# Two layers of attention and experts: row norms by a diagonal product, a first gather with a table of its own, and a later request for four weight blocks

## The reference

```python
def layer(x, mod, P, l, ctx=None):
    sh1, sc1, g1, sh2, sc2, g2 = jnp.split(mod, 6, axis=-1)
    h = rms_norm(x, P["norm_attn_pre"][l]) * (1 + sc1) + sh1
    a, new_ctx = token_mix(h, P, l, ctx)
    x = x + g1 * rms_norm(a, P["norm_attn_post"][l])
    h = rms_norm(x, P["norm_ffn_pre"][l]) * (1 + sc2) + sh2
    x = x + g2 * rms_norm(moe(h, P, l), P["norm_ffn_post"][l])
    return x, new_ctx
```

## Time and profile before

| | us |
| --- | --- |
| median of three runs | 1719.44 (1718.69 to 1720.09) |
| the profiled execution's own time | 1719.05 |
| its span, first to last instruction | 1717.2 |
| PE busy in it | 1671.3 (97%) |
| DVE, ACT, POOL busy | 432.0, 321.0, 121.2 |
| mean granted TensorE clock | 0.994 of full speed |

### The profile page before, as it was taken

How to read it: one execution, slowest core, us unless ns; L and a number is a source line. 1 busy time by engine, 2 the same in 40 slices (tenths; PEclk the granted TensorE clock), 3 DMA queues, 4 the chain that set the end, 5 groups by cost and what they waited for, 6 DMA issues and landing times. The chain is left out here.

```text
span 1717.2 us, 20998 instructions
## 1 busy us (share of the span) xinstructions
PE 1671.3 (97%) x8091; PEld 894.8 (52%) x8091; DVE 432.0 (25%) x1179; ACT 321.0 (19%) x754; POOL 121.2 (7%) x161
## 2 busy tenths in 40 slices
PE   6999999989999999999999999999899999999997
PEld 4778788543333333333367878884333333333332
DVE  1114444351111111111131444434311111111113
ACT  1010341121111111111120113402111111111111
POOL 3001000010000000001020000001100000000000
PEclk8999999999999999999999999999999999999999
DMA  9994233369999999999999632334899999999993
GB/s 388 397 407 155 87 110 129 123 233 405 424 424 424 426 425 426 425 425 425 420 392 420 263 108 98 101 137 161 305 415 427 425 426 425 423 427 423 426 426 136
DMA packets 60381, 559.87 MB, mean 326 GB/s; under 512 B 12941, under 2 KB 13089, under 8 KB 20353
## 3 DMA queue, kind: packets, MB, share of 16 engines
q1 hardware_dynamic: 45360, 529.55, 75.0%
q0 software_dynamic: 14928, 29.02, 4.9%
HBM read 576.02 MB, written 4.78 MB: 338 GB/s over the span
## 5 line engine op out<-in xcount | busy, mean ns | idle before, releaser
L1038 PE MATMUL PS<-ring,region 128*64 128x512 f32 x2048 | 450.6, 592 | 1.9 <-issue 1.5
L1038 PEld LDWEIGHTS PS<-ring,region 128*64 128x64 f32 x2048 | 147.3, 137 | 290.7 <-issue 290.6
L617 PE MATMUL PS<-region,ring 128*128 128x256 f32 x1088 | 245.4, 381 | 0.5 <-DMA ring<-in_blocks 0.5
L1085 PE MATMUL PS<-region 128*128 128x512 f32 x512 | 241.0, 594 | 0.0
L1062 PE MATMUL PS<-ring,region 128*64 128x512 f32 x1024 | 235.5, 602 | 0.2
L617 PEld LDWEIGHTS PS<-region,ring 128*128 128x128 f32 x1088 | 203.8, 190 | 34.2 <-issue 6.3
L1757 DVE SCALAR_TENSOR_TENSOR region<-region,PS 128x256 f32<-128x256 f32 x64 | 26.9, 421 | 670.6 <-ACT region L1320 670.6
L510 PEld LDWEIGHTS PS<-const,region 128*128 128x128 f32 (+1 forms) x925 | 106.8, 141 | 121.8 <-issue 74.1
L510 PE MATMUL PS<-const,region 128*128 128x128 f32 (+1 forms) x925 | 138.5, 279 | 18.2 <-DMA region<-in_c 8.7
L1062 PEld LDWEIGHTS PS<-ring,region 128*64 128x64 f32 x1024 | 68.1, 137 | 158.7 <-issue 158.0
L1324 ACT ACTIVATE region<-PS 128x512 f32<-128x512 f32 x128 | 76.4, 597 | 267.4 <-PE PS L1062 267.4
(11 more groups left out here) (260 smaller groups left out, 985.4 us busy)
## 6 DMA issues: line engine op xcount, KB each, us to landing
ring<-in_expert_blocks SPq DMA_DIRECT2D x192, 2048.0 KB, 16.7
ring<-in_blocks SPq DMA_DIRECT2D x120, 1024.0 KB, 19.7
region<-post_rows POOLq DMA_DIRECT2D x8, 512.0 KB, 5.3
h_table<-region POOLq DMA_DIRECT2D x4, 512.0 KB, 4.0
region<-in_w_kvk POOLq DMA_DIRECT2D x2, 640.0 KB, 18.2
region<-in_mla_w_ukv POOLq DMA_DIRECT2D x2, 512.0 KB, 21.4
region<-in_post_pack POOLq DMA_DIRECT2D x2, 512.0 KB, 24.7
region<-h_table,region POOLq DMA_INDIRECT x64, 10.7
```

What stands on the lines that cost most here:

```text
L617: last = pe.matmul(PS[:, j % 2, m * T:(m + 1) * T], w[:, k, m * P:(m + 1) * P], hT[:, k, :], start=(k == 0), stop=(k == KC - 1))
L1038: last = pe.matmul(PS[e * CAP:(e + 1) * CAP, 0, :], xe[:, k, e * CAP:(e + 1) * CAP], w[:, k % 4, :], start=(k == 0), stop=(k == KC - 1), s ...
L1085: last = pe.matmul(PS[:, 4 + 2 * t + half, :], hot[:, t * P:(t + 1) * P], og[:, half * HALF:(half + 1) * HALF], start=False, stop=True, sk ...
```

## The change

The change has eight parts.

1. **Products with a diagonal.** DVE no longer multiplies the rows by the root. It multiplies a 128 x 128 identity by it (`root_diagonal`), and PE makes the product of a 128 x 128 piece of x with that diagonal in place of the transpose. ACT's sums of squares are made over halves of 512 columns. Where both tiles are ready together (start of layer 1, behind the experts), their roots are made in one chain of nine steps on two columns (`both_roots`).
2. **Residual rows.** `take_gains` multiplies the PSUM rows by the gains, half by half and before the root is known; `add_rows` then multiplies by the root and adds in one instruction per half.
3. **Tile 0 earlier.** Tile 0's product with its diagonal stands inside the output projection, behind step 3 of the last group of eight.
4. **The first gather.** The rows of h are also written to a second table without gates, and the first gather reads that table and waits only for those two writes. Its gates come by a product with the 0/1 matrix that gives its row numbers. The later gathers wait for all writes (`gates_in`).
5. **The first pair's order on PE.** The lists are transposed inside the first gate-and-up product, behind its second step; the second pair's rows are transposed ahead of and around the hidden rows of the first.
6. **The shared expert** is cut at other places between router, gates and first gather.
7. **The end.** x of both tiles is stored in halves as DVE makes them; the addition on POOL is gone.
8. **The later request.** In layer 0 SP waits before block 8 until block 5 has landed.

The parts of the diff that these stand on, cut:

```diff
                 for n in range(LOADS):
+                    if l == 0 and n == L_QA[0]:
+                        sp.wait_ge(ring_in[L_MOD[1] + 1], 16)
                     load_block(n)
...
+                    pool.dma_start(first_table[P * t:P * (t + 1), :], h2x[:, t, 0:D]).then_inc(table_in, 16)
+                    pool.dma_start(table[P * t:P * (t + 1), 0:D], h2x[:, t, 0:D]).then_inc(gates_in, 16)
...
-                pool.wait_ge(table_in, (l + 1) * 64)
+                pool.wait_ge(table_in, (l + 1) * 32)
...
                         if g == 1:
+                            pool.wait_ge(gates_in, (l + 1) * 64)
                             pool.wait_ge(rows_ready, q + 1)
...
-            pool.wait_ge(last_scaled, 1)
-            pool.tensor_tensor(xr[:, 0, :], xr[:, 0, :], moe_scaled[:, 0, :], ALU.add).then_inc(last_ready, 1)
...
-                        last = transpose(PS[:, bank + c // 4, (c % 4) * P:(c % 4 + 1) * P], src[:, t, c * P:(c + 1) * P])
+                        last = pe.matmul(PS[:, bank + c // 4, (c % 4) * P:(c % 4 + 1) * P], xr[:, t, c * P:(c + 1) * P], diag[:, t, :],
+                                         start=True, stop=True)
...
+                            if t == 1 and half == 1 and k == 3:
+                                normalised(1, 0, diag2, 0)
...
+                    for t in range(2):
+                        last = pe.matmul(PS[:, 1, 2:4], first_hot[:, t, :], h2x[:, t, D:D + 2], start=(t == 0), stop=(t == 1), skip_group_check=True)
+                    last.then_inc(first_done, 1)
...
+                                if g == 0 and k == 2 and e == 0:
+                                    transpose_lists()
...
-                    transpose_lists()
                     gate_up(0)
+                    transpose_inputs(1, 0)
                     transpose_hidden(0)
-                    transpose_inputs(1, 0)
+                    transpose_inputs(1, 1)
                     down(0)
-                    transpose_inputs(1, 1)
...
+                def root_diagonal(r, t, diag):
+
+                    ve.tensor_scalar(diag[:, t, :], ident, r, ROOT_SCALE, ALU.mult, ALU.mult).then_inc(xn_ready, 1)
...
+                def take_gains(i, t, rows, rows_in):
+
                     dve.wait_ge(postb_in, (l * 2 + rows_in) * 2 * 16)
+                    for half, cols in enumerate(HALVES):
+                        dve.wait_ge(sum_done, l * SUMS + 2 * i + half + 1)
+                        step.add(ve.tensor_tensor(rows[:, t, cols], PS[:, 4 + 2 * t + half, :], postb[:, t, cols], ALU.mult))
+
+                def add_rows(r, t, rows, done):
+
+                    for half, cols in enumerate(HALVES):
+                        ve.scalar_tensor_tensor(out=xr[:, t, cols], in0=rows[:, t, cols], scalar=r, in1=xr[:, t, cols], op0=ALU.mult, op1=ALU.add).then_inc(done, 1)
```

213 lines of the change are left out of this document (118 added, 95 removed).

## The result

The changed kernel takes 1709.36 us (median of 5 runs, 1708.11 to 1710.63), the kernel before 1719.44 (5 runs): a ratio of 0.9942, 95% interval 0.9927 to 0.9956, or -10.1 us where -4.35 was forecast and 1711.8 us was the lower end of the range. The direction was right, the size was not.

The account below looks back on a forecast made before the run. PE, busy 97% of the span, was taken as the bound, with DMA also full at both layers' starts. The terms 0 - 0.95 - 1.75 + 0.45 - 2.1 = -4.35 us, from 1719.44, gave 1715.1 us; range 1711.8 to 1719.

Parts of the forecast that it names:

- Start of layer 0, 0: Layer 0 up to block 20: waits of 1.54 us swallow the longer products, the deferral is hidden; 0, bounds -0.3 to +1.
- Rival D: Start of layer 0: deferring block 8 starves the load queue, all 5 us show; +0.65 us, 1720.1 us, chance 0.05.
- First pair of layer 0, -2.5: Output projection to second pair, layer 0: fewer PE waits and the new order start the second pair at 387.8; -2.5 us.
- The second gather's lag: Second pair's rows, issued at 377.0 in layer 0: assumed to land after 5.6 us, and 6.7 us in layer 1.
- Gate products, +0.45: Last pair of each layer: the next pass's gate products also stand on PE, +0.45 us per layer.
- Start of layer 1: Block 7 to DVE's scaling: earlier landing, longer products; a lead of 2.05 us becomes 0.95, bounds 0.5 and 1.7.
- First pair of layer 1: Same steps as in layer 0, but the clock falls again; second pair at 1231.5 instead of 1233.27, -1.75 us.
- rival B: First pairs: the clock stays up in both layers; -1.65 us more, 1713.4 us, chance 0.12.
- The end, -2.1: Last stage: without POOL's addition holding DVE up, x is complete at 1712.6 instead of 1714.78; -2.1 us.
- The diagonals: Both norms: eight products with the diagonal cost PE 0.78 us more than eight transposes.
- Rival A: Layer 1's start: transfers keep PE's gain, block 7 lands as before; -3.3 us, 1716.1 us, chance 0.25.
- Rival C: First pairs: the second gather lands late (11.7 us), holding PE and down(0); +5.75 us, 1725.2 us, chance 0.05.

Follow-up runs that it names:

- e1: Changed kernel with the deferral alone undone, so block 8's request no longer waits for block 5 in layer 0: 1709.75 us, ratio 0.9940 to the kernel before.
- e4: Changed kernel with 32 idle transposes on PE ahead of the second pair of layer 0 only: 1712.69 us, ratio 0.9971 to the kernel before.
- e9: Changed kernel with the same 32 idle transposes on PE ahead of the seventeenth pair of layer 0: 1712.75 us, ratio 0.9960 to the kernel before.
- e12: Changed kernel with the first pair's first two slots given back only when the second gather has landed: 1712.95 us, ratio 0.9964 to the kernel before.
- b2: Kernel before with 14 idle transposes in PE's wait for the first pair's hidden rows, both layers: 1717.11 us, ratio 0.9990 to the kernel before.
- e5: Changed kernel with POOL adding the first tile again in the last stage: 1714.77 us, ratio 0.9974 to the kernel before.
- e11: Changed kernel with scaled rows and transposes in place of diagonals and products for both norms: 1705.84 us, ratio 0.9919 to the kernel before.
- e7: Changed kernel with scaled rows and transposes for the second norm only, in the new places: 1706.13 us, ratio 0.9924 to the kernel before.
- e3: Changed kernel with the first pair's order on PE put back to the old one: 1720.04 us, ratio 1.0002 to the kernel before.
- e2: Changed kernel without the first gather's own table; it reads the common table after the gate columns are written: 1712.37 us, ratio 0.9954 to the kernel before.
- e8: Changed kernel with the first tile's diagonal products put behind the output projection: 1714.85 us, ratio 0.9971 to the kernel before.
- e14: e3 with 18 and 14 idle transposes put into PE's two waits in the first pair: 1715.05 us, ratio 0.9974 to the kernel before.
- e10: Changed kernel with the second pair's inputs transposed behind the first pair's down product: 1716.45 us, ratio 0.9982 to the kernel before.
- e13: e11 with 5 and 4 idle transposes in the first pair's two waits: 1705.38 us, ratio 0.9916 to the kernel before.

## Why the prediction was off, point by point

In the prediction's own terms the profiles give 0 - 3.0 - 5.5 + 0.4 - 2.6 = -10.7 us for its 0 - 0.95 - 1.75 + 0.45 - 2.1 = -4.35.

- **Start of layer 0, 0:** 0.08 earlier. The landing of block 20 set it, as described, and the deferral is worth nothing (e1). Rival D did not come. But the 2.4 us that the longer products were to cost ahead of it, and that the waits were to swallow, were not put to the test. They rested on a clock at 0.50 there; in after it was 1.00 from 8 to 26 us, and each tile's products took 2.05 us. Tile 0's cost 0.1 us more than its transposes at the lower clock had, and not 1.8. The clock was up before the products began (modulation for the block ahead of them took 1.07 us, 1.94 before), so it was not the products that kept it up.
- **First pair of layer 0, -2.5:** -3.3. The stage to the first gathered rows gave 2.2 us, where the prediction had 1.2 to 1.3. It counted PE's waits of 0.77 and 0.66 us and left out three others on the way: 0.23, 0.47 and 0.36 us (the last two for ACT and for the first gather). In after one of 0.24 is left.
- **The second gather's lag, taken over from before (5.6 and 6.7 us), is the step behind both this and the largest error below.** It landed after 4.2 us in layer 0 and 4.5 in layer 1. So PE waited 0.59 us for it and not 1.6. "This wait replaces the one for the hidden rows" failed with it: there was a wait of 0.82 us for them, and they set the start of down(0), at 383.46 and not 384.25.
- **Gate products, +0.45:** from the second pair to the end of the pairs, 472.98 us before and 473.40 after: +0.42.
- **Start of layer 1, mis-sized:** the step "block 7 lands 1.2 to 2.4 us earlier; I take 1.6" failed. It landed 3.4 us earlier, as much as the second pair came earlier. The landing did not keep the first release's lead but that of the second pair's start: the queue had slack until then (DMA share 0.77 to 0.98 from 376 to 400 us in the kernel before). e4, e9 and e12 bear that out. The working behind block 7 held (6.25 us worked out, 6.13 measured to DVE's scaling). Worth 2 us.
- **First pair of layer 1, the largest error:** -5.5 within this stage where -1.75 was forecast. 2.5 us come before the first gathered rows (forecast 1.2); of the three waits left out, the one for the first gather was 0.91 us here. The step "PE's idle gap is 1.6 to 2.9 us in either layer now, and it was 2.1 in both before, so I keep each as it was" failed, through the gather's lag: there was no such gap. Before, PE stood 2.06 us without a break; after, there are 0.86 and 0.65 us with the second pair's transposes between. The clock did not fall: 1.65 us, rival B in layer 1, which had a chance of 0.12. b2 confirms that the fall in the kernel before hung on that wait: filled, it goes. That the shorter waits kept the clock here was in part luck, since it fell behind such waits in layer 1 of e5, e9 and e11. The remaining 1.3 us are the first pair's shorter work, as in layer 0.
- **The end, -2.1:** -2.6. The hold-up between POOL and DVE was seen rightly (e5).
- **The diagonals:** priced at 0.78 us a tile and inside the sums, but called covered at the start of layer 1 and outweighed elsewhere. Those of the second norm cost 3.2 us (e7), both 3.5 (e11). The prediction did not consider that one part of the change is better left out.
- **Rival A** fell with block 7's landing. **Rival C** is real, in some executions: lags of 8.7 to 9.9 us in four profiles, above the 8.1 from which it was to decide, and 6 us of time for the one execution of e1.

By medians, each part taken away alone: the order with its clock 10.7 us (e3; put into the kernel before alone it gives 5), the roots as a pair 3.4, the place inside the projection 5.5, the end without POOL 5.4, the table up to 3, the diagonals -3.2, the deferral 0. These come to far more than the 10.1. Two reasons are shown: order and earlier rows pay only together, so that each counts the same gain, and the clock fell in the profile of e3, where the removal lengthens PE's waits, and in that of e5, where it does not. Late second gathers in e2 and e8 are a third, as far as their profiles go.

## What to carry to other kernels

When an order is changed, look at each wait of TensorE by itself and at the granted clock behind it, not only at the sum: filling waits of 2 to 3 us with idle transposes was worth 5 us in e14. Do not carry a transfer's lag over from the kernel before as if it were fixed: the second gather of layer 0 took 4.1 to 9.9 us over the profiles, and rivals B and C both hung on it. For the landing at the end of a long stretch that transfers fill, what counts is how much the queue has moved by the time its last gap closes; a delay there moved the landing, one in the middle did not, though both cost the total the same where TensorE is full as well. Take the parts of a joined change away one by one: the best version here leaves one of them out, and two of them are worth their price only together.

## What the runs showed of the hardware

- The granted clock was at 0.50 behind unbroken waits of 3.05, 2.43 and 2.16 us (e3), 2.06 and 2.16 (e10), 2.06 (the kernel before, layer 1) and 5.66 (e1). It stayed at 1.00 behind 2.06 us in layer 0 of the kernel before, behind 2.07 in layer 0 of e3 and behind 1.69 in layer 1 of e7. Where two waits of 0.47 to 1.01 us stood around the second pair's transposes, it fell in 3 of 19 cases (layer 1 of e5, e9 and e11). So the wait alone does not decide it; shorter and broken waits had a fall behind them less often. A fall costs 1.7 us there, and 5 us in the kernel with several (e3 against e14).
- With float32 transposes put into the waits the clock was at 1.00 behind them, in both layers of the profiles of e14, b2 and e13. Against e3, e14 shows that the transposes did it.
- The second gather of layer 0, at the same place between the same transfers, took some 4.2 us to land in after, 5.6 in the kernel before and 9.9 in e8. What decides between them was not found; the expert load beside it may have a part in it (e12).
- A VectorE step on 512 columns took 0.69 us alone and 2.83 beside GpSimd's addition (e5).
- A piece of 128 x 128 in float32 cost two records as a product and one as a transpose: 1.95 to 2.05 us for eight products, 1.04 to 1.09 for eight transposes.
